# MLP norms: tile sums on VectorE and summed first on TensorE; latent attention's first two weight rests on VectorE

## The reference

```python
def layer_norm(x, g, b):
    mu = jnp.mean(xf, axis=-1, keepdims=True)
    var = jnp.mean(jnp.square(xf - mu), axis=-1, keepdims=True)
    y = (xf - mu) * lax.rsqrt(var + LN_EPS) * g + b

for i in range(2):                     # i = 0: latent attention, i = 1: state space mixer
    shift, scale, gate = modulation(cs, mod_mix_w[i], mod_mix_b[i])
    h = x * (1.0 + scale) + shift
    y = mla_mixer(h, ...) if i == 0 else s5_mixer(h, ...)
    x = layer_norm(ALPHA * x + (1.0 + gate) * y, ln_mix_g[i], ln_mix_b[i])
    shift, scale, gate = modulation(cs, mod_ffn_w[i], mod_ffn_b[i])
    h = x * (1.0 + scale) + shift
    y = sq_relu_mlp(h, ...)            # (relu(h @ w1 + b1) ** 2) @ w2 + b2
    x = layer_norm(ALPHA * x + (1.0 + gate) * y, ln_ffn_g[i], ln_ffn_b[i])
```

## Time and profile before

| | |
|---|---|
| median of 3 runs | 3946.09 us (3943.99 to 3948.16) |
| profiled execution | 3945.7 us, its span 3943.8 us |
| TensorE matmul busy | 3745.4 us, 95% |
| VectorE busy | 2296.6 us, 58% |
| ScalarE busy | 1647.0 us, 42% |
| GpSimd busy | 1106.7 us, 28% |

### The profile page before, as it was taken

The page is one execution under the profiler, slowest core; times in us unless marked ns, Lnnn a source line. Parts: engine busy times, 40 slices in busy tenths (PEclk is TensorE's granted clock), DMA queues, the critical chain, the costliest instruction groups (busy, mean ns, idle before and its releaser), DMA issues. The chain is left out here.

```text
span 3943.8 us, 47054 instructions
## 1 busy us (share of the span) xinstructions
PE 3745.4 (95%) x18172; PEld 3107.4 (79%) x18172; DVE 2296.6 (58%) x3601; ACT 1647.0 (42%) x2245; POOL 1106.7 (28%) x647
## 2 busy tenths in 40 slices
PE   7999899989999999999999999998999998789998
PEld 6888677768788888888888888886778886777886
DVE  6555445346366665755367777776555465855353
ACT  5555454445322234544444444445543223434222
POOL 1222122145144433333344444442020004502002
PEclk9999999899999999999999999999999999999999
DMA  4111021055234345345598888881123322132331
GB/s 178 55 53 54 12 66 47 13 187 203 68 126 131 129 128 192 123 185 201 205 297 264 265 267 264 267 259 60 35 74 103 96 96 65 32 99 75 97 96 64
DMA packets 226410, 515.87 MB, mean 131 GB/s; under 512 B 23792, under 2 KB 98800, under 8 KB 224016
## 3 DMA queue, kind: packets, MB, share of 16 engines
q1 hardware_dynamic: 203968, 408.89, 32.2%
q0 software_dynamic: 18720, 68.17, 5.3%
q10 hardware_dynamic: 3504, 35.85, 2.2%
HBM read 438.64 MB, written 69.21 MB: 129 GB/s over the span
## 5 line engine op out<-in xcount | busy, mean ns | idle before, releaser
L1330 PE MATMUL peer_banks<-peer_h_parts,peer_w_parts 128*128 128x512 f32 x3456 | 800.8, 392 | 8.5 <-DVE peer_w_parts L1785 5.1
L1330 PEld LDWEIGHTS peer_banks<-peer_h_parts,peer_w_parts 128*128 128x128 f32 x3456 | 646.5, 188 | 141.6 <-DVE peer_w_parts L1785 5.3
L1330 PE MATMUL peer_banks<-peer_act_parts,peer_w_parts 128*128 128x512 f32 x3072 | 696.8, 389 | 0.7 <-DVE peer_act_parts L1885 0.7
L1330 PEld LDWEIGHTS peer_banks<-peer_act_parts,peer_w_parts 128*128 128x128 f32 x3072 | 576.5, 188 | 120.8 <-DVE peer_w_parts L1890 1.1
L1529 POOL TENSOR_TENSOR peer_w_parts<-slots,peer_w_parts 128x1024 fp32r<-128x1024 f32 x142 | 339.9, 2394 | 579.7 <-ACT peer_w_parts L1676 579.7
L1330 PE MATMUL ffn_ps<-h_parts,ffn_w_parts 128*128 128x512 f32 x1920 | 450.7, 396 | 19.6 <-DVE h_parts L2495 11.0
L1676 ACT ACTIVATE peer_w_parts<-slots 128x1024 fp32r<-128x1024 f32 x272 | 287.0, 1055 | 386.0 <-PE peer_banks L1330 382.1
L1330 PEld LDWEIGHTS ffn_ps<-h_parts,ffn_w_parts 128*128 128x128 f32 x1920 | 364.9, 190 | 104.0 <-DVE ffn_w_parts L2339 15.6
L1330 PE MATMUL ffn_ps<-ffn_hidden,ffn_w_parts 128*128 128x512 f32 x1920 | 439.7, 391 | 2.3 <-DVE ffn_hidden L2402 2.3
L1330 PEld LDWEIGHTS ffn_ps<-ffn_hidden,ffn_w_parts 128*128 128x128 f32 x1920 | 361.5, 188 | 79.0 <-issue 3.9
L1880 DVE TENSOR_TENSOR peer_slab<-peer_slab 128x512 f32<-128x512 f32 x128 | 294.3, 2299 | 63.6 <-DMA peer_slab<-peer_gates 63.6
(11 more groups left out here) (553 smaller groups left out, 5447.3 us busy)
## 6 DMA issues: line engine op xcount, KB each, us to landing
slots<-in_peer_u SPq DMA_DIRECT2D x128, 512.0 KB, 3.6
slots<-in_peer_v SPq DMA_DIRECT2D x128, 512.0 KB, 4.8
slots<-in_mlp_w SPq DMA_DIRECT2D x128, 512.0 KB, 3.5
peer_slab<-in_w_mod POOLq DMA_DIRECT2D x96, 512.0 KB, 4.2
peer_acts<-h SPq DMA_DIRECT2D x128, 256.0 KB, 2.4
peer_gates<-peer_slab ACTq DMA_DIRECT2D x16, 2048.0 KB, 16.6
peer_slab<-peer_acts SPq DMA_DIRECT2D x128, 256.0 KB, 5.2
peer_slab<-peer_gates SPq DMA_DIRECT2D x128, 256.0 KB, 5.5
```

Source lines behind the costliest of these rows:

```text
L1330: last = nc.tensor.matmul(out, w(a, k), x(b, k), start=start and k == ks[0] and n == 0, stop=stop and k == ks[-1] and n == 2)
```

## The change

Two edits. In the MLP norms the tile sums (`rest`) move from GpSimd to VectorE, ahead of residual tile 7, and TensorE does the last tile's pair of matmuls directly behind that of `rest`, before that of `total`. In latent attention weight rests 0 and 1 move from GpSimd to VectorE, behind its first two scalings, with a semaphore of their own (`zw_first`); the waits of TensorE and SP follow.

```diff
             def statistics(j):
                 pe.wait_ge(rest_done, j + 1)
                 M(s1[:], K.ones[:], rest[:], start=True, stop=False)
+                pe.wait_ge(*centered(j, KT - 1))
+                M(s1[:], K.ones[:], K.h[:, KT - 1, :], start=False, stop=True).then_inc(sum_done, 1)
                 pe.wait_ge(sq_added, (j + 1) * (KT - 2))
                 M(s2[:], K.ones[:], total[:], start=True, stop=False)
-                pe.wait_ge(*centered(j, KT - 1))
-                M(s1[:], K.ones[:], K.h[:, KT - 1, :], start=False, stop=True).then_inc(sum_done, 1)
...
-            def add_rest(j, k):
-                eng.wait_ge(*centered(j, k))
-                ins = G.tensor_tensor(rest[:], K.h[:, 4, :] if k == 5 else rest[:], K.h[:, k, :], ALU.add)
...
                 add_square(j, 4)
-                add_rest(j, 5)
                 add_square(j, 5)
-                add_rest(j, 6)
                 add_square(j, 6)
...
+            def add_rest(j):
+                dve.wait_ge(*centered(j, 5))
+                st.then(V.tensor_tensor(rest[:], K.h[:, 4, :], K.h[:, 5, :], ALU.add))
+                dve.wait_ge(*centered(j, 6))
+                V.tensor_tensor(rest[:], rest[:], K.h[:, 6, :], ALU.add).then_inc(rest_done, 1)
...
+            add_rest(0)
             residual_tile(0, 7)
...
+            add_rest(1)
             residual_tile(1, 7)
...
-            sp.wait_ge(zw_lo, 1)
+            sp.wait_ge(zw_first, 1)
             sp.dma_start(raw[:, 0, :], d["mla_win"][4]).then_inc(K.win_in[0], 16)
             for s in range(1, 4):
-                sp.wait_ge(zw_lo, s + 1)
+                sp.wait_ge(*((zw_first, 2) if s == 1 else (zw_lo, s - 1)))
...
-            for t in range(ZT):
+            for t in range(2, ZT):
                 eng.wait_ge(zw_hi, t + 1)
                 G.tensor_tensor(zw[:, t, 1, :], raw[:, t % 4, :], zw[:, t, 0, :].bitcast(F32), ALU.subtract).then_inc(zw_lo, 1)
...
-            pe.wait_ge(zw_lo, 2)
+            pe.wait_ge(zw_first, 2)
...
             scale(0)
+            scale(1)
+            for t in range(2):
+                dve.wait_ge(zw_hi, t + 1)
+                V.tensor_tensor(zw[:, t, 1, :], raw[:, t, :], zw[:, t, 0, :].bitcast(F32), ALU.subtract).then_inc(zw_first, 1)
             for k in range(KT):
-                if k + 1 < KT:
+                if 2 <= k + 1 < KT:
                     scale(k + 1)
```

More of the change, by code:

```diff
@@ L2639, in mla @@
         banks = ph.banks("banks", 8)
+        zw_first = ph.sems("z_w_first_lo")
         (small, zw_hi, zw_lo, e_done, h_hi, h_full, h_lo, z_done, pos_in, ang_done, trig_done, rope_done, sq_done, sum_done, rstd_ready,
@@ L2671, in _ @@
                 sp.dma_start(wts[:, h, :], d["mla_wh"][h]).then_inc(wt_in[h], 16)
-            sp.wait_ge(zw_lo, 1)
+            sp.wait_ge(zw_first, 1)
             sp.dma_start(raw[:, 0, :], d["mla_win"][4]).then_inc(K.win_in[0], 16)
             for s in range(1, 4):
-                sp.wait_ge(zw_lo, s + 1)
+                sp.wait_ge(*((zw_first, 2) if s == 1 else (zw_lo, s - 1)))
                 sp.dma_start(raw[:, s, :], d["mla_wo"][s]).then_inc(K.slots.ready[s], 16)
-            sp.wait_ge(zw_lo, ZT)
+            sp.wait_ge(zw_lo, ZT - 2)
             sp.dma_start(raw[:, 0, :], d["mla_wo"][0]).then_inc(K.slots.ready[0], 16)
@@ L2711, in _ @@
             for t in range(2, ZT):
-                pe.wait_ge(zw_lo, t + 1)
+                pe.wait_ge(zw_lo, t - 1)
                 for k in range(KT):
```

## The result

| | before | after |
|---|---|---|
| median | 3946.03 us (4 runs, 3943.99 to 3948.16) | 3922.28 us (4 runs, 3919.43 to 3923.95) |
| profiled execution | 3945.7 us, span 3943.8 | 3919.43 us, span 3917.5 |
| ratio, 95% interval | | 0.994 (0.9927 to 0.9954) |

The change takes 23.75 us off the median, 0.6%. That lies inside the stated range; the forecast of 3926.5 us was 4.2 us too slow.

A forecast was written before the change was run, and what follows sets the result against it. TensorE, busy 95%, bounds the kernel; only its waits or low clock can give time. 5.2 + 5.1 + 5.3 + 0.6 + 1.8 = 18.0 us, plus 1.6 for one restart, gives 19.6: median 3926.5 us, range 3920.5 to 3934.

The forecast's parts named there:

- VectorE's additions: Tile sums moved to VectorE in the MLP norms: two additions per norm, taken at 1.1 us each.
- rival (b): In the norms, the square chain of GpSimd and ScalarE keeps the time: 14.1 us gained, 3932.0 us; chance 0.18.
- A and C: First norms (j = 0) of the first and second MLP phases: gains of 5.2 and 5.3 us.
- Two of my own signs: Signs of being right or wrong: tile sum within 1 us of the last product; additions above 1.2 us mean wrong.
- the upper of my two cases: First norm of the first MLP phase: gain 5.5 us with the sums at the high clock, 4.9 at the low.
- B: Second norm (j = 1) of the first MLP phase: a gain of 5.1 us, bounds 4.7 and 5.5.
- D: Second norm (j = 1) of the second MLP phase: a gain of 0.6 us, bounds 0.4 and 0.9.
- Latent attention: Start of latent attention, first two weight rests on VectorE: 1.8 us gained, bounds 0.5 and 1.9.
- The clock at the restart: Weights restarting behind three norms: each gives back 0 to 1.6 us; one of three taken, 1.6 us.
- rival (a): Weight restarts behind three norms all run at the high clock: 22.8 us gained, 3923.3 us; chance 0.16.
- (c): In the norms, TensorE's release does not move and only matmul order counts: 4.2 us gained, 3941.9 us; chance 0.04.
- (d): Behind the norms' sums, the clock stays at 1.2 GHz through spares and first weight group: slower, 3977 us; chance 0.04.

The follow-up runs named there:

- e7: The changed kernel with the first of VectorE's two tile-sum additions per norm made one product earlier; 3922.25 us, ratio 0.9939.
- e8: The changed kernel with GpSimd's rest of weight tile 3 in latent attention held back until all eight low parts are made; 3919.97 us, ratio 0.9938.
- e5: The kernel before with 72 instead of 56 spare matmuls behind the sums of three norms; 3939.6 us, ratio 0.9986.
- e2: The kernel before with only the norms' part of the change, latent attention as before; 3926.78 us, ratio 0.9949.
- e3: The kernel before with only the norms' tile sums moved to VectorE, TensorE's old order kept; 3935.91 us, ratio 0.9973.
- e4: The kernel before with only TensorE's new order in the norms, tile sums still on GpSimd; 3937.9 us, ratio 0.9977.
- e10: e3 with spare matmuls, which nobody reads, in TensorE's waits in two norms, A and C; 3935.12 us, ratio 0.9971.

## Why the prediction was right, point by point

- **What bounds the kernel, and where the time can come from**: right. The 23.3 us counted above come from TensorE's waits or its low clock at the five places and right behind three of them.
- **VectorE's additions**: mis-sized. I took 1.1 us each from L2368; they took 1.78 and 1.63 (A), near the 1.75 that I had given to rival (b). Rival (b) made A and C 1.9 us shorter in gain from that, and this did not happen. The step that failed in (b) is that GpSimd would pay for it too: its fourth square sum came 0.3 us later against the last product than before, not 0.9 or 1.8. (b) also took the low clock in the sums, and it stayed at 1.00. What I missed is what 1.12 us meant: both moves that took it ended 0.55 us behind GpSimd's square sum, having begun late in it. The additions begin early in one, and so cost more. The row was in the trace before the change. Two of my own signs came out against me here: the additions took more than 1.2 us, and the tile sum was there 1.9 us behind the last product in A, not within 1 us. The reading that the mean waits for ScalarE's last square, not for TensorE, was right, and e7 shows it: with the sum 1.6 us earlier the mean does not move in A, and in C, where both had ended within 0.1 us of each other, it moves by 0.1.
- **A and C**: 5.70 and 5.46 us against 5.2 and 5.3 (bounds 4.9 to 5.6). The mean came 6.4 us earlier in A; I had 5.6. The clock stayed high in the sums, the upper of my two cases; e8, where it fell in A, lost 0.95 us there.
- **B**: 4.42 us against 5.1, below my lower bound of 4.7. I had both additions over before the product ends. They took 1.78 and 1.67 us, the last residual and the first pair were pushed back by some 0.4 us, and the variance came 9.53 us behind the high part where I had 8.92. e7, which takes the first addition away from there, gives 4.89. And 1.6 of the 4.42 us are luck of the profile before, whose pairs in B ran in part at the low clock: against e5's 20.01 the gain is 2.8.
- **D**: 0.57 us against 0.6.
- **Latent attention**: 2.10 us against 1.8, above my bound of 1.9. I had TensorE's start 4.55 us behind ScalarE's first instruction, and it was 4.38: the two rests took 2.35 us, and I had 2.5.
- **The sum of these**: 18.3 us against 18.0. It is this close because B's shortfall of 0.7 and the 1.0 more of A, C and latent attention nearly cancel.
- **The clock at the restart**: the term that failed. I took one restart of three, 1.6 us, and all three stayed at 2.4 GHz, 5.0 us, of which 1.8 lie behind B, where the scan blurs the figure. That is rival (a), to which I gave 0.16; its 3923.3 us is 1.0 us from the median. What I missed is that the gap is made at both its ends. Before, the variance started 0.5 us behind the last pair, since it waited for the mean; after, it starts at once. And from the variance to the restart it is 7.6 us instead of 8.0, since the scalings meet less of GpSimd. Both shorten the gap, from 2.3 to 1.4 us in A. I had written that it hardly changes in A and C if the sums run at the high clock. My own times for A were enough to see otherwise: the total from 2900.5, 1.7 us for two pairs and 6.41 for the spares make 2908.6, the restart 5.5 us before 2915.78 is 2910.3, and the gap 1.7 us. I did not work it out. For B I had the sums 3.6 us and the norm 5.1 us earlier, which makes the gap 1.5 us shorter, and I wrote about one; it went from 2.31 to 1.47.
- **Order and tile sums**: I costed them one behind the other and had no term for what they do together. e2, e3, e4 and e10 show one: 4.7 us of the norms' gain come only with both, and some 3.5 of them are clock, as e10 shows: the new order leaves TensorE no second long wait in A and C, and the clock stays up. The rest is not taken apart.
- **Rivals (c) and (d)**: (c) needs TensorE to be released no earlier; it was. (d) needs the clock low through the spares and the group behind them; in all thirteen profiles the spares of A, B and C run at 1.00. My argument against (d), that the clock was back at the restart of A, was a misreading: it was back in the spares (56 in 6.41 us), and at the restart it fell to 0.60.

## What to carry to other kernels

When a critical chain on a slow engine is relieved, look for the next one by name; here it was the neighbouring chain of square sums, and speeding up what was no longer late (e7) gave nothing in A and C. Order TensorE's pieces so that what is ready first fills the wait for what is not, since a wait can cost twice, once as time and once as the low clock behind it. Before moving work to VectorE, look which GpSimd instruction will run when it starts, and charge it what is left of that. And when a forecast moves a stage's start and end by different amounts, work out the idle gap that is left ahead of the next burst: here that gap was worth a quarter of the work's gain.

## What was not expected of the hardware

- Two additions of two SBUF inputs beside GpSimd's own: 1.78 and 1.63 to 1.68 us on VectorE instead of 0.68, each ending 0.55 us behind GpSimd's instruction. GpSimd pays much less. Its five square sums in A took 1.82, 1.56, 1.53, 1.54 and 1.27 us; the first two took 1.81 and 1.55 before the change as well, so the two additions cost it 0.5 us in all, where I had 0.9.
- The clock at a restart, over the first 4 us of the weights behind A, B and C in thirteen profiles: 1.00 at all 25 restarts behind a gap of 0.5 to 1.7 us, and 0.57 to 0.68 at all 14 behind a gap of 1.8 to 2.9 us. I had expected it to depend more on chance. This is the boundary at these restarts alone: ahead of the sums, waits of 1.95 to 2.15 us were followed by either clock.
- The same instructions can run at either clock: in B two of the four pairs took 1.8 and 2.1 us before, and all four took 1.02 to 1.12 in e5, which changes nothing in them.
